# Moving the first tile of the normalised rows and the merged rows to the weights' byte place modulo 512

## The reference, cut to what matters

```python
def rms_norm(x, g):
    y = xf * lax.rsqrt(jnp.mean(xf * xf, axis=-1, keepdims=True) + NORM_EPS)
    return (y * g.astype(jnp.float32)).astype(x.dtype)
...
h = rms_norm(x, g_mix[l])
proj = h @ w_in[l]
...
merged = gates[:, :, 0] * y_a + gates[:, :, 1] * y_b + gates[:, :, 2] * y_c + gates[:, :, 3] * y_d
x = x + merged @ w_merge[l]
h2 = rms_norm(x, g_ffn[l])
gt = causal_dwconv(h2 @ w_ffn_gate[l], ffn_conv_w[l])
x = x + (jax.nn.silu(gt) * (h2 @ w_ffn_up[l])) @ w_ffn_down[l]
```

## Time and profile before

| | us |
|---|---|
| median of 3 runs | 1798.43 |
| the runs | 1796.06 to 1802.86 |
| the profiled execution, its own time | 1797.66 |
| span of the profiled execution | 1795.9 |

### The profile page before, as it was taken

One profiled execution on the slowest core, in us unless ns is written; L12 is line 12 of the kernel. 1 busy time (PEld: TensorE's weight loads), 2 busy tenths in 40 slices (PEclk: granted clock), 3 DMA queues, 4 the chain that ended last, 5 costly groups with the idle time before them and its releaser, 6 DMA issues.

```text
span 1795.9 us, 31735 instructions
## 1 busy us (share of the span) xinstructions
PE 1738.4 (97%) x13416; PEld 1641.0 (91%) x13416; DVE 1226.3 (68%) x1927; ACT 932.3 (52%) x1291; POOL 125.0 (7%) x35
## 2 busy tenths in 40 slices
PE   6999999999999999999999998889999999999998
PEld 6989999899989999999999898769998999889986
DVE  6994956797649868467887475977554656666553
ACT  5446655454445546654644356756443655655432
POOL 1620300000004503000000000000000000000000
PEclk9899999999999999999999989989999999999999
DMA  7684546556554554546465555415555486436551
GB/s 232 183 204 132 188 135 207 165 176 197 192 198 156 182 168 126 187 158 217 142 201 185 184 160 146 142 48 164 192 185 200 166 213 160 130 119 210 188 199 70
DMA packets 248636, 305.75 MB, mean 170 GB/s; under 512 B 9266, under 2 KB 223630, under 8 KB 248495
## 3 DMA queue, kind: packets, MB, share of 16 engines
q1 hardware_dynamic: 235959, 289.66, 49.3%
q10 hardware_dynamic: 12536, 14.06, 4.2%
HBM read 299.51 MB, written 4.19 MB: 169 GB/s over the span
## 4 chain that ended last, share of the span: by engine, by line
PE 76%; DVE 15%; ACT 4%; DMA 3%; issue 2%; DVEq 0%; ACTq 0%; SPq 0%
PE psum L471 23%; PE psum L472 22%; PE psum L473 22%; DVE wlo L447 3%; DVE psum L1482 3%; DMA raw<-in_w_in 1%; DVE work L1614 1%; PE psum L2483 1%; PE psum L2509 1%; DVE work L1612 1%; DMA raw<-in_a_w_in 1%; PE psum L2495 1%; ACT whi L439 1%; DMA raw<-in_b_w_q 1%; DVE work L1628 1%
## 5 line engine op out<-in xcount | busy, mean ns | idle before, releaser
L439 ACT ACTIVATE whi<-raw 128x2048 fp32r<-128x2048 f32 (+2 forms) x277 | 525.1, 1901 | 370.8 <-PE psum L473 261.3
L447 DVE TENSOR_TENSOR wlo<-raw,whi 128x2048 fp32r<-128x2048 f32 x249 | 566.8, 2281 | 198.0 <-PE psum L473 164.4
L471 PE MATMUL psum<-hT,whi 128*128 128x256 f32 x2160 | 608.2, 282 | 2.9 <-DVE wlo L447 1.5
L472 PE MATMUL psum<-hT,whi 128*128 128x256 f32 x2160 | 604.8, 280 | 0.0
L473 PE MATMUL psum<-hT,wlo 128*128 128x256 f32 x2160 | 604.7, 280 | 0.0
L471 PEld LDWEIGHTS psum<-hT,whi 128*128 128x128 f32 x2160 | 410.8, 190 | 4.2 <-DVE wlo L447 2.2
L472 PEld LDWEIGHTS psum<-hT,whi 128*128 128x128 f32 x2160 | 407.4, 189 | 0.2
L473 PEld LDWEIGHTS psum<-hT,wlo 128*128 128x128 f32 x2160 | 407.4, 189 | 0.0
L447 POOL TENSOR_TENSOR wlo<-raw,whi 128x2048 fp32r<-128x2048 f32 (+1 forms) x28 | 123.8, 4423 | 575.5 <-ACT whi L439 396.0
L471 PE MATMUL psum<-whi,hidden 128*128 128x512 f32 x352 | 137.2, 390 | 1.0 <-issue 1.0
L473 PE MATMUL psum<-whi,hidden 128*128 128x512 f32 x352 | 137.0, 389 | 0.0
(11 more groups left out here) (367 smaller groups left out, 3073.1 us busy)
## 6 DMA issues: line engine op xcount, KB each, us to landing
raw<-in_w_in SPq DMA_DIRECT2D x78, 1024.0 KB, 5.5
raw<-in_ffn_w_up SPq DMA_DIRECT2D x44, 1024.0 KB, 5.0
raw<-in_w_ffn_gate SPq DMA_DIRECT2D x22, 1024.0 KB, 5.1
raw<-in_w_ffn_up SPq DMA_DIRECT2D x22, 1024.0 KB, 5.2
raw<-in_w_ffn_down SPq DMA_DIRECT2D x22, 1024.0 KB, 4.8
raw<-in_ffn_w_down SPq DMA_DIRECT2D x22, 1024.0 KB, 4.9
raw<-in_b_w_q SPq DMA_DIRECT2D x12, 1024.0 KB, 6.0
raw<-in_a_w_in SPq DMA_DIRECT2D x10, 1024.0 KB, 5.1
```

Of the source, the lines that this page charges most:

```text
L439: act.activation(part(whi, n, HIGH_SLOTS), part(raw, n, RAW_SLOTS), ACT.Copy).then_inc(high_made, 1)
L447: eng.tensor_tensor(part(wlo, n, LOW_SLOTS), part(raw, n, RAW_SLOTS), part(whi, n, HIGH_SLOTS).bitcast(F32), ALU.subtract).then_inc(stream ...
L471: nc.tensor.matmul(dst, left[0], right[0], start=first, stop=False)
L472: nc.tensor.matmul(dst, left[0], right[1], start=False, stop=False)
```

## The change

`hT` is taken apart. Tile 0 of its high and low part lie at the start of `h_place`, that is at byte 128 modulo 512; tiles 1 to 7 of both lie behind them and `LEAD_ROWS`, at byte 64 as before. `hT` becomes a list of 8 views for each part, and `row_tile` picks a tile from a list or from a tensor. `joined` moves to the start of `h_place`, from byte 0 to byte 128. Nothing else is touched: the same instructions on the same data, in the same order, with the same waits.

```diff
-        hT_both = over("hT", at_h, LEAD_ROWS, [2, KT, S])
-        hT = [hT_both[:, i] for i in range(2)]
-        joined_both = over("joined", at_h, LEAD_ROWS - 16, [2, KT, S])
+        first_tiles = over("hT_first", at_h, 0, [2, 1, S])
+        other_tiles = over("hT", at_h, 2 * S + LEAD_ROWS, [2, KT - 1, S])
+        hT = [[(other_tiles[:, i, k - 1, :] if k else first_tiles[:, i, 0, :]) for k in range(KT)] for i in range(2)]
+
+        def row_tile(v, k):
+
+            return v[k] if isinstance(v, list) else v[:, k, :]
+
+        joined_both = over("joined", at_h, 0, [2, KT, S])
         joined = [joined_both[:, i] for i in range(2)]
...
                     mm = three_passes(b[:, j * S:(j + 1) * S], [v[:, k, j * P:(j + 1) * P] for v in w],
-                                      [v[:, k, :] for v in src], k == 0, k == KT - 1)
+                                      [row_tile(v, k) for v in src], k == 0, k == KT - 1)
...
-                ins = act.activation(dst[0][:, 2 * b + j, :], bank(base + b)[:, j * S:(j + 1) * S], ACT.Copy,
+                ins = act.activation(row_tile(dst[0], 2 * b + j), bank(base + b)[:, j * S:(j + 1) * S], ACT.Copy,
                                      scale=gain(2 * b + j))
...
-                                mm = three_passes(b[:, j * S:j * S + wd], [v[:, k, j * P:(j + 1) * P] for v in hT],
+                                mm = three_passes(b[:, j * S:j * S + wd], [row_tile(v, k)[:, j * P:(j + 1) * P] for v in hT],
                                                   [v[:, k, 0:wd] for v in w], k == 0, k == KT - 1)
```

More of the change, by code:

```diff
@@ L624, in whole_low @@
             for j in range(2):
-                ins = dve.scalar_tensor_tensor(dst[1][:, 2 * b + j, :], bank(base + b)[:, j * S:(j + 1) * S],
-                                               gain(2 * b + j), dst[0][:, 2 * b + j, :].bitcast(F32),
+                ins = dve.scalar_tensor_tensor(row_tile(dst[1], 2 * b + j), bank(base + b)[:, j * S:(j + 1) * S],
+                                               gain(2 * b + j), row_tile(dst[0], 2 * b + j).bitcast(F32),
                                                ALU.mult, ALU.subtract)
@@ L1114, in dense @@
                                 mm = three_passes(b[:, j * S:(j + 1) * S], [v[:, k, j * P:(j + 1) * P] for v in w],
-                                                  [v[:, k, :] for v in (rows if n < RAW else hT)], k == 0, k == KT - 1)
+                                                  [row_tile(v, k) for v in (rows if n < RAW else hT)], k == 0, k == KT - 1)
                             else:
-                                mm = three_passes(b[:, j * S:j * S + wd], [v[:, k, j * P:(j + 1) * P] for v in hT],
+                                mm = three_passes(b[:, j * S:j * S + wd], [row_tile(v, k)[:, j * P:(j + 1) * P] for v in hT],
                                                   [v[:, k, 0:wd] for v in w], k == 0, k == KT - 1)
@@ L1872, in dense_half @@
                             mm = three_passes(b[:, j * S:(j + 1) * S], [v[:, k, j * P:(j + 1) * P] for v in w],
-                                              [v[:, k, :] for v in hT], k == 0, k == KT - 1)
+                                              [row_tile(v, k) for v in hT], k == 0, k == KT - 1)
                     if j:
@@ L2466, in dense_half @@
                             mm = three_passes(b[:, j * S:(j + 1) * S], [v[:, k, j * P:(j + 1) * P] for v in w],
-                                              [v[:, k, :] for v in (hT if n < KV else mix_T)], k == 0, k == KT - 1)
+                                              [row_tile(v, k) for v in (hT if n < KV else mix_T)], k == 0, k == KT - 1)
                     if j:
```

## The result

The changed kernel takes **1786.89 us** (median of four runs, 1785.56 to 1788.95) against 1799.37 for the kernel before in the same comparison: a ratio of 0.9937, 95% interval 0.9917 to 0.9957. The profiled execution took 1786.2 us, its span is 1784.4. In a later comparison the same two kernels stood at 1783.73 and 1801.97 (ratio 0.9899, interval 0.9884 to 0.9915), so the gain lies between some 12 and 18 us. The two intervals do not overlap, and no run shows why.

A forecast was written before the change was run, and what follows sets the result against it. TensorE was taken as the bound: number of matmuls times start-to-start distance, plus waits. Gains of 2.0 + 14.1 + 4.4 + 1.6 = 22.1 us gave 1776 us against the median 1798.43; whole range 1770 to 1806, the forecast's own 1770 to 1783.

The forecast's parts named there:

- `joined`, 2.0 us: Product with the merged rows: moving them to byte 128 takes 384 matmuls from 232.1 to 226.8 ns, 2.0 us gained.
- The first tile sets the short distance: Normalised rows: three matmuls per group of 24 at the weights' place pull the rest to 113.2 ns; chance 0.40.
- The gross of 14.1 us: Four FFN-up stages: 3204 long matmuls on `hT` each gain 4.4 ns, all on the path.
- Equal places pull the lock into the short state: Read from the `hidden` product: with both TensorE streams at one byte place, matmuls settle at 0.39 us within eight.
- what the three matmuls cost themselves: First tile's three matmuls in each group of 24: taken as nothing, with bounds of nothing and 17 ns.
- The nearest row above: At 95.17 us a tile of weights streams while weights are loaded; four starts take 17 ns more than four short ones.
- Other long rows, 4.4 us: `hT` moving outside the FFN-up stages: 1656 long matmuls worth 7.3 us, six tenths counted because TensorE waits there.
- `hT` loaded, 1.6 us: Where `hT` is the loaded operand: 864 matmuls, three quarters long by 4.1 ns, 2.7 us, six tenths counted.
- What is late next: FFN-up stage: VectorE keeps most of its idle time, and weight DMAs deliver a 1024 KB unit in 5.43 us.
- The flip: Rival, chance 0.25: every first tile switches `hT` matmuls between short and long, leaving half the groups long; 1791.6 us.
- The long lock: Rival, chance 0.22: the first tile sets the long distance in every group on `hT`; slower, 1808 us.
- That places do nothing: Rival, chance 0.03: byte places have no effect, `hidden` and `joined` differ by their stage; 1798.4 us, no change.

## Why the prediction came out as it did

- **`joined`, 2.0 us: right**, term and mechanism; 226.7 ns and all durations at 389.
- **The first tile sets the short distance: right** in all four FFN-up stages, from the second or third group on; they are 12.0 us shorter. The gross of 14.1 us was sound too (15.1 with the stage's ends). The reason was wrong. "Equal places pull the lock into the short state" was read from `hidden`, which has 512 columns; at 256 columns equal places run at 120.0 ns, and it is leaving them that starts the short distance. That the sign came out was in part luck.
- **The step that failed: what the three matmuls cost themselves ("I take nothing, as a lock that holds needs no second switch").** It costs 20 ns a group, to the tile and back, although the short state holds before and behind it. Over 270 groups that is 5.4 us, half of the 10.9 us by which the forecast was low. The nearest row above, 17 ns at the swap, was nearly the price, though no run shows that the two have one cause (other placements paid 27 to 53 ns); it was kept for a rival, and the end "nothing" was taken from `hidden`, which makes no change of place in a group.
- **Other long rows, 4.4 us: 1.8 measured.** 2968 matmuls are 124 groups, by 20 ns 2.5 us; 4.4 - 2.5 is 1.9, about what came. The share of six tenths fits, the price was missing again.
- **`hT` loaded, 1.6 us: wrong.** With the weights moving, the first tile keeps the state that it finds. In the mixer's stretch from 75.8 us the profiled execution has 118.3 ns a matmul by the starts, 0.5 above the long distance; the second execution of the same kernel has 114.2 there, short and with the 20 ns to pay:

```profile
L477 PE MATMUL psum<-whi,hT x48: 279/279/284, 76.2 to 95.0; 128*128 128x256 f32 x48
...
L477 PE MATMUL psum<-whi,hT x48: 275/276/277, 75.9 to 94.0; 128*128 128x256 f32 x48
```

- With the price in and the term of `hT` loaded at nothing the sum is 22.1 - 5.4 - 1.6 = 15.1 us; 14.0 and 15.5 were measured in the two executions.
- **What is late next: right.** VectorE still waits 20.3 us in 13 waits for the product in the FFN-up stage (25.7 in 14 before); no DMA became the bound.
- **The rivals.** The flip had a price and came nearest in time in the first comparison (1791.6), but no stage alternates between 276 and 281 ns. The long lock did not come where `hT` moves. That places do nothing is refuted by 113.3 and 120.0 ns for the same instruction at offsets of 64 and 0. The Trainium skill, page "TensorE: Matmul & The Clock Gate", section "Step-by-step: what each phase is for", has the load of the next weights take no read bandwidth from the running matmul. If nothing else tied the two together, places would do nothing; the distances here disagree with that, as the earlier trace rows did, though no run shows that it is the reads that meet. The measured time lies inside the whole range and above the forecast's own 1770 to 1783, between the forecast and the flip.

## What to carry to other kernels

Where TensorE is the bound and starts follow each other without a gap, compare the distance of equal shapes in several stages: 4.4 ns in 113.3 were worth 15 us in the FFN-up stages here, and no engine's idle time shows it. Look at where the moving operand and the loaded one lie against each other, modulo 128 bytes, and try to set the state once, ahead of a long stage without pauses, rather than in every group. When a price has a bound on both sides, and the row at the lower end has another shape, take the one whose shape is the same.

## What the runs showed of the hardware that was not expected

- For 256 columns of float32r, rows moving, the distance depends on the offset of the moving operand against the loaded weights modulo 128 bytes: 113.3 or 117.8 ns at 64, 118.2 to 119.3 at 32, 48, 80 and 96, 118.6 to 120.0 at 0.
- For 512 columns, with the weights moving, it is 226.7 where the two are equal modulo 512, 229 to 233 at an offset of 64 modulo 128, and 232.1 to 233 where they are equal modulo 128 but lie 128 bytes apart modulo 512.
- At the offset of 64, for 256 columns, there are two lasting distances, and a stage of 864 matmuls kept the one that it came in with, but for one that a pause turned from short to long. One matmul in 24 at equal places is enough to bring it to the short one, within its first unit or two.
- Three matmuls in a row at a place equal modulo 512 cost 20 ns a group, one alone, or two apart, 27, six 40; three at a place equal modulo 128 alone 53.
- Why this is so no run shows; that it lies in how the two streams are read together is only argued, from its dependence on the offset of both.
